# A 32x32 inverse, products made ahead and two strings in an RWKV-7 recurrence on TensorE

## What is computed

```python
def step(S, inp):
    r_t, w_t, k_t, v_t, a_t, b_t = inp
    sa = jnp.einsum('bhvk,bhk->bhv', S, a_t)
    S = S * w_t[:, :, None, :] + sa[..., None] * b_t[:, :, None, :] + v_t[..., None] * k_t[:, :, None, :]
    return S, jnp.einsum('bhvk,bhk->bhv', S, r_t)
```

## Time and profile before

| | |
|---|---|
| Median of 3 runs | 1660.3 us (1658.23 to 1662.76) |
| The profiled execution | 1661.37 us |
| Its span in the trace | 1659.6 us |
| TensorE's mean granted clock | 0.992 of full speed |
| Time mixing, groups (524.5 to 548.5 us) | 24.0 us |
| Levels (548.5 to 594.6 us) | 46.1 us |
| Recurrence up to the last `out_open` (594.6 to 625.1 us) | 30.5 us |

### The profile page before, as it was taken

How to read it: one execution, slowest core, us unless ns; L and a number is a source line. 1 busy time by engine, 2 the same in 40 slices (tenths; PEclk the granted TensorE clock), 3 DMA queues, 4 the chain that set the end, 5 groups by cost and what they waited for, 6 DMA issues and landing times.

```text
span 1659.6 us, 27774 instructions
## 1 busy us (share of the span) xinstructions
PE 1624.7 (98%) x11505; PEld 1387.9 (84%) x11505; DVE 1250.4 (75%) x1178; ACT 977.4 (59%) x987; POOL 103.2 (6%) x151
## 2 busy tenths in 40 slices
PE   9999999999998999999999999999999999999997
PEld 7879999999677985788888888888888888888886
DVE  5655655545676734788988988988898988998987
ACT  5665434431433222667767767677676767767765
POOL 3463000001003100000000000000000000000000
PEclk9999999999999999999999999999999999999999
DMA  8115555542430006499999999999999999999994
GB/s 283 52 52 180 177 177 178 178 158 78 152 137 17 4 4 241 159 374 378 360 358 349 372 355 382 365 349 356 367 366 375 363 350 357 368 364 377 362 367 187
DMA packets 191617, 432.68 MB, mean 261 GB/s; under 512 B 10051, under 2 KB 11075, under 8 KB 191492
## 3 DMA queue, kind: packets, MB, share of 16 engines
q1 hardware_dynamic: 191452, 430.82, 72.6%
q10 hardware_dynamic: 40, 0.08, 0.0%
HBM read 429.82 MB, written 1.05 MB: 260 GB/s over the span
## 4 chain that ended last, share of the span: by engine, by line
PE 93%; DVE 4%; ACT 2%; issue 1%; ACTq 0%; POOL 0%; DVEq 0%; POOLq 0%
PE ps L1377 18%; PE ps L1379 18%; PE ps L1378 18%; PE ps L711 6%; PE ps L713 6%; PE ps L712 6%; PE ps L960 4%; PE ps L1270 2%; PE ps L1401 1%; PE ps L1093 1%; PE ps L1108 1%; PE ps L970 1%; PE ps L1330 1%; DVE arena L2210 1%; DVE wsplit L2393 0%
## 5 line engine op out<-in xcount | busy, mean ns | idle before, releaser
L2393 DVE TENSOR_TENSOR wsplit<-raw_w,wsplit 128x2048 fp32r<-128x2048 f32 x336 | 751.3, 2286 | 78.5 <-ACT wsplit L1813 78.5
L1813 ACT ACTIVATE wsplit<-raw_w 128x2048 fp32r<-128x2048 f32 x336 | 624.9, 1919 | 59.4 <-PE ps L1379 59.4
L1377 PE MATMUL ps<-wsplit,xsplit 128*128 128x512 f32 x896 | 354.2, 395 | 0.0
L1379 PE MATMUL ps<-wsplit,xsplit 128*128 128x512 f32 x896 | 349.5, 390 | 0.0
L1378 PE MATMUL ps<-wsplit,xsplit 128*128 128x512 f32 x896 | 348.9, 389 | 0.0
L1379 PEld LDWEIGHTS ps<-wsplit,xsplit 128*128 128x128 f32 x896 | 168.1, 188 | 35.8
L1378 PEld LDWEIGHTS ps<-wsplit,xsplit 128*128 128x128 f32 x896 | 168.5, 188 | 33.2
L1377 PEld LDWEIGHTS ps<-wsplit,xsplit 128*128 128x128 f32 x896 | 168.3, 188 | 33.4 <-DVE wsplit L2393 0.5
L1377 PE MATMUL ps<-wsplit,hsplit 128*128 128x512 f32 x448 | 175.2, 391 | 1.5 <-DVE hsplit L2423 1.5
L1378 PE MATMUL ps<-wsplit,hsplit 128*128 128x512 f32 x448 | 174.4, 389 | 0.0
L1379 PE MATMUL ps<-wsplit,hsplit 128*128 128x512 f32 x448 | 174.4, 389 | 0.0
(11 more groups left out here) (415 smaller groups left out, 2247.3 us busy)
## 6 DMA issues: line engine op xcount, KB each, us to landing
raw_w<-in_moe_w_gate SPq DMA_DIRECT2D x114, 1024.0 KB, 7.1
raw_w<-in_moe_w_up SPq DMA_DIRECT2D x112, 1024.0 KB, 7.8
raw_w<-in_moe_w_down SPq DMA_DIRECT2D x112, 1024.0 KB, 7.2
ffn_raw<-in_ffn_w_up SPq DMA_DIRECT2D x14, 1024.0 KB, 5.2
ffn_raw<-in_ffn_w_gate SPq DMA_DIRECT2D x14, 1024.0 KB, 5.1
ffn_raw<-in_ffn_w_down SPq DMA_DIRECT2D x14, 1024.0 KB, 5.1
ffn_raw<-in_attn_w_qkv SPq DMA_DIRECT2D x6, 1024.0 KB, 11.1
ffn_raw<-in_attn_w_o SPq DMA_DIRECT2D x4, 1024.0 KB, 11.1
```

The costliest lines, as they stand in the source:

```text
L1377: mm(o, x_[0], w_[0], start=first_, stop=False)
L1379: return mm(o, x_[1], w_[0], start=False, stop=last_)
L1813: A(wsplit[:, m % NRING, 0, :], raw_w[:, m % NRAW, :], ACT.Copy).then_inc(w_hi, 1)
L2393: v.tensor_tensor(wsplit[:, m % NRING, 1, :], raw_w[:, m % NRAW, :], wsplit[:, m % NRING, 0, :].bitcast(F32), ALU.subtract).then_inc(w_lo, 1)
```

## The change

- The inverse is kept as 32x32 blocks on the diagonal (`A32`, `X`, `XTc`, 32 columns per head where there were 64), for three levels in chunk 0 and four in the others. `level_y` and `level_x` become 32 matmuls each, 32x32, on the four diagonal tiles of the array. For chunks 1 to 4 a last level joins two blocks to 64x64 (`whole_diagonal` and one product in Y and in X); for chunk 0 it is `whole_diagonal` alone.
- `A32` comes from a new group AA (`diagonal`, 32 matmuls). DVE masks it, adds the unit, makes the first step and transposes it ahead of BA and KA; BA of chunk 0 is gone. DVE's order in a chunk is now AA, unit, first step, transpose, BA, KA.
- Two more groups, RV (K V of a chunk, kept over `KAa`) and KV (K' V, kept over `k_a`), are made one chunk behind and evicted by ACT. `rhs_values`, `state_open` and `state_values` are gone.
- In the recurrence even and odd pairs are two strings. `rhs_state`, `solve` and `state_u` are called once for each, 8 matmuls a time. DVE adds RV to both halves of the right hand side and `Sd` to both halves of the state; ACT evicts both halves of U. DVE makes `Sd` by a multiplication and then an addition of KV. Chunk 0 has no right hand side to evict.
- POOL builds seven masks of 32 columns in the place of masks 2 to 7.
- In attention, five products of the identity with itself (`filler`, 128x128) stand before `values(c)` for c = 0 to 5.

The diff, cut to its core:

```diff
+mask32 = mask64[:, 2:6, :].rearrange("p a (b i) -> p (a b) i", i=CH // 2)
+M_STRICT, M_LEVEL, M_FIRST, M_UNIT = 0, 1, 5, 6
...
+X, XTc = [area(X4 + 7168 + n * 1280, PAIRS * NCH, CH // 2) for n in range(2)]
 XS = wk + 4608
+A32 = area(XS + 1280, PAIRS * NCH, CH // 2)
...
-NLV = [3] + [5] * (NCH - 1)
+N32 = [3] + [4] * (NCH - 1)
+NLV = [n + 1 for n in N32]
...
+    GROUPS += [(kind, c) for kind in ("AA", "BA", "KA", "TB", "TK", "TV")
+               if not (c == NCH - 1 and kind in ("TB", "TK") or c == 0 and kind == "BA")]
+    if c:
+        GROUPS += [("RV", c - 1), ("KV", c - 1)]
+GROUPS.append(("RV", NCH - 1))
...
+        if c < 6:
+            filler(5, 6)
...
+    def diagonal(c):
+        b = group("AA", c)
+        for p, e, rows, toks in heads:
+            for k in range(2):
+                t = slice(c * CH + 32 * k, c * CH + 32 * (k + 1))
+                o = ps[ROWS32[2 * tok(p, e) + k], b + p % 2, (p // 2) * 32:(p // 2 + 1) * 32]
+                last = mm(o, b_a[rows, p, t], kk_a[rows, p, t], start=True, stop=True)
+        last.then_inc(grp_mm, 1)
...
+    def from_values(kind, c):
+        b = group(kind, c)
+        pe.wait_ge(grp_dve, EVICTED[G["KA", c]][1])
+        pe.wait_ge(grp_act, EVICTED[G["TV", c]][1])
+        for p, e, rows, toks in heads:
+            if kind == "RV":
+                last = mm(quarter(b, p, toks), KAa[c][toks, p, :], v_a[toks, p, cs_(c)], start=True, stop=True)
+            else:
+                last = mm(quarter(b, p, rows), k_a[toks, p, cs_(c)], v_a[toks, p, cs_(c)], start=True, stop=True)
...
-        products("BA", c)
+        diagonal(c)
+        if c:
+            products("BA", c)
         products("KA", c)
         if c < NCH - 1:
             turned("TB", c)
             turned("TK", c)
         turned("TV", c)
+        if c:
+            from_values("RV", c - 1)
+            from_values("KV", c - 1)
+    from_values("RV", NCH - 1)
...
+        if l < N32[c]:
+            for p in range(PAIRS):
+                for rows in ROWS32:
+                    last = mm(ps[rows, n % 4, p * 32:(p + 1) * 32], A32[rows, c * PAIRS + p, :], X[rows, c * PAIRS + p, :],
+                              start=True, stop=True)
+        else:
+            whole_diagonal(l, c)
+            for p in range(PAIRS):
+                for h in range(2):
+                    upper, lower = ROWS32[2 * h], ROWS32[2 * h + 1]
+                    last = mm(ps[lower, n % 4, p * 32:(p + 1) * 32], BAa[c][upper, p, 32:CH], X[upper, c * PAIRS + p, :],
+                              start=True, stop=True)
+        last.then_inc(y_mm, 1)
...
+                wide_ = CH if c == 0 else 32
+                mm(ps[upper, 4 + n % 4, p * CH:p * CH + wide_], X[upper, c * PAIRS + p, :],
+                   ident[upper, h * CH:h * CH + wide_], start=True, stop=True)
+                last = mm(ps[lower, 4 + n % 4, p * CH:(p + 1) * CH], X[lower, c * PAIRS + p, :],
+                          ident[lower, h * CH:(h + 1) * CH], start=True, stop=True)
...
+            if l < N32[c]:
+                for rows in ROWS32:
+                    last = mm(ps[rows, 4 + n % 4, p * 32:(p + 1) * 32], XTc[rows, c * PAIRS + p, :], Y[rows, c, p, :],
+                              start=True, stop=True)
+            else:
+                for h in range(2):
+                    upper, lower = ROWS32[2 * h], ROWS32[2 * h + 1]
+                    last = mm(ps[upper, 4 + n % 4, p * CH + 32:(p + 1) * CH], Y[lower, c, p, :],
+                              XTc[lower, c * PAIRS + p, :], start=True, stop=True)
...
+    by_y = [[h for h in heads if h[0] % 2 == y] for y in range(2)]
+    def rhs_state(c, y):
+        pe.wait_ge(s_ok, 2 * c - 1 + y)
+        for p, e, rows, toks in by_y[y]:
+            last = mm(quarter(0, p, toks), kk_a[rows, p, cs_(c)], S[(c - 1) % 2][rows, p, :], start=True, stop=True)
+        last.then_inc(rhs_mm, 1)
...
+            pe.wait_ge(rhs_ev, 2 * c - 1 + y)
+        for p, e, rows, toks in by_y[y]:
+            last = mm(quarter(2, p, toks), XT[toks, c * PAIRS + p, :], (RHS if c else KAa[0])[toks, p, :], start=True, stop=True)
...
+        pe.wait_ge(u_ev, 2 * c + y + 1)
+        for p, e, rows, toks in by_y[y]:
+            last = mm(quarter(4, p, rows), b_a[toks, p, cs_(c)], U[c % 2][toks, p, :], start=True, stop=True)
...
-    rhs_values(0)
-    for c in range(3):
-        if c:
-            rhs_state(c)
-            if c == 1:
-                out_open()
+    for c in range(NCH):
+        for y in range(2 if c else 0):
+            rhs_state(c, y)
+        if c in (1, 2):
+            if c == 2:
+                pe.wait_ge(own_mm, own_at["u", 1])
             out_state(c)
-        state_open(c)
-        solve(c)
-        state_values(c)
-        if c:
+        for y in range(2):
+            solve(c, y)
+        if c in (1, 2):
             pe.wait_ge(own_mm, own_at["out", c])
             out_values(c, (0, 1))
-        state_u(c)
-        if c:
+        if c < NCH - 1:
+            for y in range(2):
+                state_u(c, y)
+        if c == 0:
+            out_open()
+        elif c < 3:
             last = out_u(c, (0, 1))
-            if c == 2:
+            if c == 1:
+                signal_own(last, ("u", c))
+            else:
                 last.then_inc(ot_mm, 1)
-        rhs_values(c + 1)
-    rhs_state(3)
-    state_open(3)
-    solve(3)
-    state_values(3)
-    state_u(3)
-    rhs_values(4)
-    rhs_state(4)
-    solve(4)
...
+        for kind, n, dst in (("RV", c - 1, KAa[c - 1]), ("KV", c - 1, k_a[:, :, cs_(c - 1)])) if c else ():
+            g = G[kind, n]
+            act.wait_ge(grp_mm, g + 1)
+            A(by_parity(dst), two_banks(2 * (g % 4)), ACT.Copy).then_inc(grp_act, 1)
...
-        act.wait_ge(rhs_mm, c + 1)
-        A(evens(RHS), quad(0), ACT.Copy).then_inc(rhs_ev, 1)
-        act.wait_ge(u_mm, c + 1)
-        A(evens(U[c % 2]), quad(2), ACT.Copy).then_inc(u_ev, 1)
-        if c < NCH - 1:
-            act.wait_ge(s_mm, c + 1)
-            A(evens(S[c % 2]), quad(4), ACT.Copy).then_inc(s_ok, 1)
+        for y in range(2):
+            act.wait_ge(u_mm, 2 * c + y + 1)
+            A(of_parity(U[c % 2], y), quad(2 + y), ACT.Copy).then_inc(u_ev, 1)
...
+        g = G["AA", c]
+        dve.wait_ge(grp_mm, g + 1)
+        strict = mask32[:, M_STRICT, :].unsqueeze(1).unsqueeze(1).to_broadcast([P, 2, 4, 32])
+        own.done(v.tensor_tensor(by_parity(A32[:, cc, :]),
+                                 ps[:, 2 * (g % 4):2 * (g % 4) + 2, 0:P].rearrange("p y (q i) -> p y q i", q=4), strict,
+                                 ALU.mult), grp_dve)
+        own.settle()
+        own.done(v.tensor_tensor(A32[:, cc, :], A32[:, cc, :], over32(M_UNIT), ALU.add), dve_own)
+        own.settle()
+        own.done(v.tensor_tensor(XTc[:, cc, :], A32[:, cc, :], over32(M_FIRST), ALU.mult), dve_own)
+        own.settle()
+        v.transpose(X[:, cc, :].rearrange("p a b -> p (a b)"), XTc[:, cc, :].rearrange("p a b -> p (a b)")).then_inc(x0_ok, 1)
...
+                if l < N32[c]:
+                    v.tensor_tensor(Y[:, c, :, :], got, over32(M_LEVEL + l), ALU.mult).then_inc(y_ev, 1)
+                else:
+                    v.tensor_copy(Y[:, c, :, :], got).then_inc(y_ev, 1)
...
-        dve.wait_ge(rhs_mm, c + 1)
-        v.tensor_copy(odds(RHS), quad(1)).then_inc(rhs_ev, 1)
+        for y in range(2 if c else 0):
+            dve.wait_ge(rhs_mm, 2 * c - 1 + y)
+            v.tensor_tensor(of_parity(RHS, y), of_parity(KAa[c], y), quad(y), ALU.add).then_inc(rhs_ev, 1)
         if c == 3:
             gn_sums(0)
-        if c == 4:
+        if c == NCH - 1:
             gn_scaled(0)
-        dve.wait_ge(u_mm, c + 1)
-        v.tensor_copy(odds(U[c % 2]), quad(3)).then_inc(u_ev, 1)
-        if c == NCH - 1:
             break
-        dve.wait_ge(s_mm, c + 1)
-        v.tensor_copy(odds(S[c % 2]), quad(5)).then_inc(s_ok, 1)
+        for y in range(2):
+            dve.wait_ge(s_mm, 2 * c + y + 1)
+            kept = Sd if c else k_a[:, :, cs_(0)]
+            v.tensor_tensor(of_parity(S[c % 2], y), of_parity(kept, y), quad(4 + y), ALU.add).then_inc(s_ok, 1)
         if c + 1 < NCH - 1:
             dve.wait_ge(s_ok, 2 * c + 2)
-            v.tensor_tensor(Sd[:, :, :], S[c % 2][:, :, :],
-                            chunkdecay[:, :, c + 1:c + 2].to_broadcast([P, PAIRS, CH]), ALU.mult).then_inc(xt_sd_dve, 1)
+            own.done(v.tensor_tensor(Sd[:, :, :], S[c % 2][:, :, :],
+                                     chunkdecay[:, :, c + 1:c + 2].to_broadcast([P, PAIRS, CH]), ALU.mult), dve_own)
+            own.settle()
+            own.done(v.tensor_tensor(Sd[:, :, :], Sd[:, :, :], k_a[:, :, cs_(c + 1)], ALU.add), dve_own)
+            own.settle()
```

More of the change, by code:

```diff
@@ L598, in _ @@
                 compact(j)
-            for l in range(2, 7):
+            compact32(M_STRICT, wide)
+            for l in range(2, 6):
                 b = 1 << (l - 1)
@@ L612, in _ @@
             unit()
-            compact(7)
```

(48 more changed lines are left out.)

102 lines of the change are left out of this document (57 added, 45 removed).

## The result

The changed kernel takes **1707.8 us** (median of 4 runs, 1706.14 to 1711.45) against 1661.53 us for the kernel before on the same chip (4 runs, 1658.23 to 1662.82): ratio 1.028, 95% interval 1.027 to 1.030. Forecast was 1642, range 1632 to 1660. It is slower by 46 us where 19 us less were forecast. The profiled execution spans 1705.7 us against 1659.6.

What follows compares the result with a forecast made beforehand. PE was taken to bound the kernel, busy 1624.7 of 1659.6 us. Terms -16.3 + 7.1 - 9.3 - 2.0 + 1.6 = -18.9 took 1661.4 to 1642.5, on the median 1641.4, stated as 1642; 80% range 1632 to 1660.

Steps and rivals of the forecast that it cites:

- step 1, the levels: Levels of the inverse: 2432 records on 32x32 tiles at 8 ns each replace 23 levels of 64 records; -16.3 us.
- The prediction's own sign of being wrong: Levels: about 8 ns a record expected; a row of 320 records taking over 4 us would show the forecast wrong.
- Step 2, the groups: Groups before the levels: DVE's new order, with KA last, leaves it idle between chunks; 31.1 in place of 24.0, +7.1 us.
- the ring: Groups: TV must wait for KA's banks (group g - 4), leaving DVE idle 1.9 us for each of chunks 2 to 4.
- Step 3, the recurrence: Recurrence: work removed and two strings bring states 4.9 us apart, 21 us against 30.5; -9.3 us.
- Step 4, attention: Attention: fillers cost about 1.5 us but avoid two stretches at the lower clock; -2.0 us.
- Step 5, the clock in the recurrence: Recurrence: light PE work, half on two tiles, brings one more stretch at 1.2 GHz; +1.6 us (0 to +7).
- The one on four row groups: Rival, levels and AA: four row groups don't overlap, 29 ns a record, levels +44, total 1707 us; chance 0.08.

## Why the prediction was wrong

**What failed is step 1, the levels:** "So 2432 x 8 = 19.5 us". The rate is right as the rate of the array: 8.6 ns in the run with the wide products. It was read as the rate of the stream. I had asked how fast tiles take records and never how fast PE gets them., from which I took that records can start this closely, has 16 records in a row after a wait of 1.32 us: a burst out of what had been delivered already. The 15 ns of `products` is read from a short burst too, 64 records. The rows of 160 at 29 ns are held by their tiles and would not have told. But the kernel before had the mark itself, in its groups, where the prediction names only PE's waits for DVE (timeline of PE, before):

```profile
527.93 0.52 PE L1064 MATMUL ps<-wide,arena 64*64 64x64 f32 x21 [1.24 <-issue]
...
531.66 0.52 PE L1064 MATMUL ps<-arena 64*64 64x64 f32 x21 [0.82 <-issue]
...
535.38 0.99 PE L1064 MATMUL ps<-arena 64*64 64x64 f32 x53 [0.58 <-issue]
```

These waits for issue are 3.73 and 3.72 us apart, with 128 records from each to the next. The prediction's own sign of being wrong came at once: the first 320 records of the levels took from 558.30 to 566.26, 8 us, where over 4 was to upset it. By count, with the rate measured since, the sum would have been 3022 x 29.6 = 89.5 us, +43.4 in place of -16.3; this is 59.7 of the 65 us between forecast and result.

**Step 2, the groups:** +7.1 forecast, +13.2 measured, and for another reason. The gaps of DVE that I expected at 1.9 us are there once at 1.91, then at 3.57, 3.73 and 4.30; but they are not the ring's. PE waits for instructions: 1312 records x 28.4 ns. With DVE's order undone nothing changed. Of the 576 records more, 288 are AA less the old BA of chunk 0, which the version with the old inverse does without (groups 28.9 to 30.1 us), and 288 are RV and KV.

**Step 3, the recurrence:** right, but for a slip: 21 against 30.5 is -9.5, and the sum has -9.3. Forecast 21 us and 4.9 us from state to state; at the full clock the version with the old inverse took 20.8 and 21.0. DVE's timeline of it, state additions:

```profile
597.44 0.75 DVE L2274 TENSOR_TENSOR arena<-arena,ps 128x256 f32<-128x256 f32 x2 [6.29 <-PE ps L1179]
...
602.37 0.75 DVE L2274 TENSOR_TENSOR arena<-arena,ps 128x256 f32<-128x256 f32 x2 [1.93 <-PE ps L1179]
...
607.29 0.75 DVE L2274 TENSOR_TENSOR arena<-arena,ps 128x256 f32<-128x256 f32 x2 [1.93 <-PE ps L1179]
```

4.93 and 4.92 us apart; the chain through `Sd`, the right hand side, `solve` and `state_u` was priced right. In the changed kernel the first steps ran at 1.2 GHz and were 6.0 us apart, 23.0 us in all. But part of the gain only moved: RV and KV take 288 records in the groups, about 5 to 6 us there (24.0 to 28.9 and 30.1), and the recurrence lost 350. Step 2 had put the groups' whole loss on AA's order, and saw no price for them.

**Step 4, attention:** -2.0 forecast, -3.4 here, with PEclk 1.00 in both stretches of the earlier trace rows. The comparison of medians gives the fillers about -2. The clock was half right: in nine profiles with fillers the second low stretch never came, the first came twice; with the fillers alone it was at 1.2 GHz through all of 70 to 80 us in the profiled execution. How much of the 2 us is the clock was not taken apart.

**Step 5, the clock in the recurrence:** +1.6 forecast; 23.0 - 20.9 = 2.1 measured, but as a tail of the levels' idle time and not from the recurrence's own work, since in the version with the old inverse the clock stayed up there.

**The rivals.** The one on four row groups named 1707 us and the right place, and its mechanism is refuted (8.6 ns): its 29 ns came from rows that two tiles hold for 58 ns each, and is the rate of the supply by chance. So the 1707 is a hit by luck. The rules that stood beside it fare no better. The Trainium skill (TensorEngine Tiling, Gotcha 1: PSUM Pressure) has different row tiles kept from one bank; four wrote one bank here at 8.6 ns a record. The Trainium skill's floor of some 25 ns between starts (TensorE: Matmul & The Clock Gate, "Wait — 56ns, not 53.3ns?") is not seen in bursts, which had 8.6 to 10 ns on different tiles; as the mean over a whole stretch of groups or levels no run here went below 27.9 ns (36.58 us for 1312 records, groups of the run with wide products). I gave the number 0.08 because its mechanism had a row against it, and looked for no other mechanism with the same number. Two things pointed at one: the count of instructions would double in the levels, and the page has a queue named "instruction" whose bytes could be divided by it.

**What stays open:** whether the 3.75 us per 16 KB is the transfer's own cycle or something in PE's queue. The transfers themselves took about 1 us (1.9% of 16 engines x 18 us, over 5, is 1.1), so it is not bandwidth. That the size of a portion and the size of a transfer agree, one per portion, is observed; it was not varied.

## What to carry to other kernels

Before splitting matmuls into smaller ones, count them: a stretch of a thousand records or more took at least 28 to 30 ns for each here, whatever they did, and a burst of some 100 records says nothing of that. Where long rows already stand at 29 ns, only fewer instructions with more columns each help, or work moved to where PE's records are long; idle time of PE put down to "issue" in portions of 127 or 128 records is the mark of it. And if a rival gives a number by a mechanism that you have refuted, ask what else would give the same number.

## What was not expected of the hardware

- PE got 128 matmul records with their weight loads per about 3.75 us wherever it could have worked faster: 29.4 to 30.0 ns a record over the 1806 to 3090 of the levels on 32x32 tiles in five kernels, 27.9 to 28.5 over the 1312 of the groups in four of them.
- A 64x64 tile is held 55 to 60 ns by a record of one column as by one of 64; a 128x128 tile 113 ns by one of 64; a 32x32 tile 34 ns by one of 32 and 56 ns by one of 64. All are on operands of type f32, where each product makes two records.
- 40 us of work on the whole array in PE's idle time cost 2.1 us in the levels.
- A wait on a semaphore met long before took PE some 50 ns.
- The lower clock through 90 us of levels cost nothing there, since PE was waiting anyway: 89.5 us with it, 91.5 with the clock up for most of them and the 76 records of the wide products.
